# Two schedules for the first projection of a fused decoder trunk: which engine sums the early modulation columns, and in which order the V items run

## The reference, cut to what matters

```python
mod = silu(c) @ ada_w[l] + ada_b[l]                  # (1, 6*1024): shift, scale, gate, twice
sh1, sc1, g1, sh2, sc2, g2 = split(mod, 6)
h = rms_norm(x, norm_mix_g[l]) * (1 + sc1) + sh1     # needs 2048 columns of mod
z = h @ w_in                                         # u, v, bg, cg, hb: 512 columns each
v = layer_norm(gelu(v), ln_g, ln_b)                  # spatial gating unit
s = einsum('hts,bnshd->bnthd', tril(w_s), v) + b_s
```

## Time and profile before

| | |
|---|---|
| median of 3 runs | 1753.85 us (1752.15 to 1755.49) |
| the profiled execution | 1755.49 us |
| its span, first to last instruction | 1753.7 us |
| TensorE busy | 1528.2 us, 87% |
| VectorE busy | 803.5 us, 46% |
| mean granted TensorE clock over the span | 0.939 |

### The profile page before, as it was taken

One profiled execution on the slowest core, in us unless ns is written; L12 is line 12 of the kernel. 1 busy time (PEld: TensorE's weight loads), 2 busy tenths in 40 slices (PEclk: granted clock), 3 DMA queues, 4 the chain that ended last, 5 costly groups with the idle time before them and its releaser, 6 DMA issues. The chain is left out here.

```text
span 1753.7 us, 16992 instructions
## 1 busy us (share of the span) xinstructions
PE 1528.2 (87%) x5419; PEld 847.6 (48%) x5420; DVE 803.5 (46%) x1496; ACT 260.8 (15%) x517; POOL 214.2 (12%) x388
## 2 busy tenths in 40 slices
PE   5989999989965999989579899977998388999992
PEld 3764544458853444444234344432887244444440
DVE  2561786644244233222225999966233522332323
ACT  3210000001131111111131000004112111111113
POOL 2000000000000232312200000000000112233320
PEclk9999999999986999999889999998999589999996
DMA  9553165560155788888462344442003758769866
GB/s 333 177 189 102 65 213 189 178 206 24 49 194 189 203 252 234 263 259 235 95 190 61 84 105 118 115 105 84 24 25 130 278 182 252 212 168 278 259 168 215
DMA packets 194671, 293.99 MB, mean 168 GB/s; under 512 B 11925, under 2 KB 153329, under 8 KB 194624
## 3 DMA queue, kind: packets, MB, share of 16 engines
q1 hardware_dynamic: 172256, 214.33, 38.5%
q0 software_dynamic: 18800, 65.39, 14.8%
q10 hardware_dynamic: 3568, 13.63, 2.1%
HBM read 240.13 MB, written 53.10 MB: 167 GB/s over the span
## 5 line engine op out<-in xcount | busy, mean ns | idle before, releaser
L913 PE MATMUL bank<-HTR,W 128*128 128x512 f32 x1024 | 454.1, 601 | 14.1 <-DVE R L1631 7.2
L1042 PE MATMUL bank<-W,R 128*128 x784 | 354.4, 606 | 23.2 <-DMA W<-in_moe_w_down 19.3
L913 PEld LDWEIGHTS bank<-HTR,W 128*128 128x128 f32 x1024 | 194.4, 192 | 252.4 <-issue 245.6
L1206 DVE TENSOR_TENSOR R<-bank,R 128x256 f32<-128x256 f32 (+1 forms) x91 | 49.3, 542 | 493.6 <-ACT R L706 296.4
L1042 PEld LDWEIGHTS bank<-W,R 128*128 128x128 f32 x784 | 148.5, 195 | 194.5 <-issue 194.5
L991 PE MATMUL bank<-W,R 128*128 128x256 f32 x1024 | 231.8, 385 | 9.0 <-ACT R L810 7.8
L991 PEld LDWEIGHTS bank<-W,R 128*128 128x128 f32 x1024 | 195.1, 193 | 38.7 <-ACT R L810 8.7
L1644 DVE SCALAR_TENSOR_TENSOR R<-R,PT 128x998 f32<-128x998 f32 (+21 forms) x152 | 195.5, 1286 | 5.4
L1057 PE MATMUL bank<-W,R 128*128 x408 | 185.4, 597 | 3.9 <-DVE R L1459 3.9
L1224 DVE SCALAR_TENSOR_TENSOR W<-W,CAB 128x256 f32<-128x256 f32 x280 | 135.7, 485 | 10.0
L1057 PEld LDWEIGHTS bank<-W,R 128*128 128x128 f32 x408 | 74.1, 192 | 78.7 <-issue 78.7
(11 more groups left out here) (200 smaller groups left out, 960.4 us busy)
## 6 DMA issues: line engine op xcount, KB each, us to landing
W<-in_ada_w SPq DMA_DIRECT2D x48, 1024.0 KB, 11.8
W<-in_moe_w_gate SPq DMA_DIRECT2D x32, 1024.0 KB, 6.8
W<-in_moe_w_up SPq DMA_DIRECT2D x32, 1024.0 KB, 11.7
W<-in_moe_w_down SPq DMA_DIRECT2D x32, 1024.0 KB, 14.0
W<-glu_scratch SPq DMA_DIRECT2D x48, 258.0 KB, 4.5
W<-in_conf_w SPq DMA_DIRECT2D x12, 1024.0 KB, 9.1
W<-in_hyb_w_in SPq DMA_DIRECT2D x10, 1024.0 KB, 12.0
xsum_scratch<-X ACTq DMA_DIRECT2D x8, 1024.0 KB, 4.1
```

The source lines that it names most:

```text
L913: ins = pe.matmul(dst[:], lhs(k), rhs(k), start=(k == 0), stop=(k == kc - 1))
L1042: ins = pe.matmul(M[0][:], XT[:, k, :], W[:, bass.ds(at + k * 2 * FE, 2 * FE)], start=(k == 0), stop=(k == KC - 1))
L1206: return dve.tensor_tensor(o, a, b, op)
```

## The change

Three things are edited together.

1. Of the early items, only the odd ones (scale columns) stay on TensorE. The even ones (0, 2, 4, 6) are summed by VectorE with `ada`: item 0 ahead of `rms_apply(0, 0)`, items 2, 4 and 6 in the steps q = 0, 1, 2 ahead of the finishes of that step. `param_columns` stays behind TensorE's first `ada_rows`, which is now that of item 1. The products of all early items go to bank 1.
2. The V groups run weight item by weight item: all 256-token blocks with WV, then all with WV+1. The transposes of the second half of the tokens come ahead of group 2. Four `a` items stand beside WV and four beside WV+1 (none beside WCG), so one is reduced after every V group. In the ring WV+1 moves behind items 8 to 11, and item 15 ahead of WCG.
3. GpSimd no longer waits for the early products before it issues the four loads of the spatial gating unit (256 KB each).

```diff
-    _k = {WV: 3, WV + 1: 4, WCG: 1, WHB: 5, ...}.get(_w, 0)
+    _k = {WV: 4, WV + 1: 4, WHB: 5, ...}.get(_w, 0)
...
-ITEMS += [("w", WV), ("w", WV + 1)] + [("a", n) for n in BESIDE[WV] + BESIDE[WV + 1]]
-for _w in range(WCG, NW0):
+for _w in range(NW0):
     ITEMS += [("w", _w)] + [("a", n) for n in BESIDE[_w]]
-VORDER = [(_j, 2 * _h + _n) for _h in range(2) for _j in range(2) for _n in range(2)]
...
-USED0 = [GROUPS["v"] + 6, GROUPS["v"] + 8]
-USED0 += [GROUPS[_g] + 4 * (_j + 1) for _g in ("cg", "hb", "bg", "u") for _j in range(2)]
+USED0 = [GROUPS[_g] + 4 * (_j + 1) for _g in ("v", "cg", "hb", "bg", "u") for _j in range(2)]
...
 def by_pe(n):
-    return n < NADA0
+    return n < NADA0 and n % 2 == 1
...
-            pool.wait_ge(ada_mm, NADA0)
             pool.dma_start(SGW, i["sgu_w"][0].rearrange("h t s -> t h s")).then_inc(sgu_in, 16)
...
             for q in range(4):
-                ada_rows(2 * q)
+                ada_rows(2 * q + 1)
                 if q == 0:
                     param_columns()
                 transposes(0, 0, ks=(2 * q, 2 * q + 1))
                 reduce_ada(2 * q)
-                ada_rows(2 * q + 1)
                 reduce_ada(2 * q + 1)
-            for m, (j, n) in enumerate(VORDER):
...
+            def v_of(g, w, n):
+                if g == GROUPS["v"] + 2:
                     transposes(0, 1)
                 ht_ready(0, n // 2)
-                rows_of(GROUPS["v"] + m, HTR, slot(at), n)
...
+                rows_of(g, HTR, w, n)
+            for j in range(2):
+                item0(WV + j, GROUPS["v"] + 4 * j, v_of)
+                if j == 0:
                     sgu_columns()
...
             def ada(n):
                 at = item_at("a", n)
                 wait_item(dve, at)
-                dve.wait_ge(red, n - 1)
+                if n == 0:
+                    dve.wait_ge(ca_ok, 1)
+                    dve.wait_ge(pt_ok, 4)
+                if n >= 2:
+                    dve.wait_ge(red, n - 1)
...
+            ada(0)
             rms_apply(0, 0)
             for q in range(4):
+                if q < 3:
+                    ada(2 * q + 2)
                 ada_finish(2 * q)
                 ada_finish(2 * q + 1)
                 evict_ht(0, 0, 0, 0, (2 * q + 1,))
```

More of the change, by code:

```diff
@@ L56 @@
 for _w in range(NW0):
-    _k = {WV: 3, WV + 1: 4, WCG: 1, WHB: 5, WHB + 1: 5, WBG: 5, WBG + 1: 5, WU: 4, WU + 1: 4, NW0 - 1: 4}.get(_w, 0)
+    _k = {WV: 4, WV + 1: 4, WHB: 5, WHB + 1: 5, WBG: 5, WBG + 1: 5, WU: 4, WU + 1: 4, NW0 - 1: 4}.get(_w, 0)
     BESIDE.append(list(range(_n, _n + _k)))
@@ L118, in by_pe @@
 def by_pe(n):
-    return n < NADA0
+    return n < NADA0 and n % 2 == 1
 def summed(n):
-    return n - NADA0 + 1
+    return n // 2 + 1 if n < NADA0 else n - NADA0 // 2 + 1
 def emptied(g):
@@ L386, in wait_used @@
             if kind == "a" and by_pe(n):
-                eng.wait_ge(ada_mm, n + 1)
+                eng.wait_ge(ada_mm, n // 2 + 1)
             elif kind == "a":
@@ L736, in x_pieces, with rows_out @@
                                    scale=RSTD[:, b:b + 1]).then_inc(xn_ok, 1)
-            def rows_out(n):
-                act.wait_ge(ada_mm, n + 1)
-                if n >= 2:
+            def rows_out(k):
+                n = k + 1
+                act.wait_ge(ada_mm, n // 2 + 1)
+                if n >= 3:
                     act.wait_ge(red, n - 1)
[L744 to L748, removed]
+                act.activation(ACC[1], M[1][:, 0:QW], ACT.Copy).then_inc(rows_ev, 1)
             rms_sums(0, 0)
-            evict_ht(0, 0, 0, 0, both_rows_out)
+            evict_ht(0, 0, 0, 0, rows_out)
             rms_sums(0, 1)
-            for m, (j, n) in enumerate(VORDER):
-                if m == 4:
+            for n in range(8):
+                if n == 2:
                     evict_ht(0, 0, 0, 1)
-                c, b = QW * j, 2 * n
+                c, b = QW * (n // 4), 2 * (n % 4)
                 act.activation(V[:, b:b + 2, c:c + QW],
-                               take(GROUPS["v"] + m)[:].rearrange("p (b c) -> p b c", b=2),
+                               take(GROUPS["v"] + n)[:].rearrange("p (b c) -> p b c", b=2),
                                ACT.Gelu).then_inc(free["A"], 1)
@@ L846, in ada_rows @@
                 wait_item(pe, item_at("a", n))
-                if n == 0:
+                if n == 1:
                     pe.wait_ge(ca_ok, 1)
-                elif n >= 2:
-                    pe.wait_ge(rows_ev, n - 1)
+                else:
+                    pe.wait_ge(rows_ev, n // 2)
                 w = slot(item_at("a", n))
@@ L853, in ada_rows @@
                     c = 32 * (k % 4)
-                    ins = pe.matmul(M[1 + n % 2][c:c + 32, 0:QW], CAB[:, k, :], w[:, k, :], start=(k < 4),
+                    ins = pe.matmul(M[1][c:c + 32, 0:QW], CAB[:, k, :], w[:, k, :], start=(k < 4),
                                     stop=(k >= 4))
@@ L860, in reduce_ada @@
                 if by_pe(n):
-                    pe.wait_ge(rows_ev, n + 1)
+                    pe.wait_ge(rows_ev, n // 2 + 1)
                 else:
@@ L865, in reduce_ada @@
                     pe.wait_ge(pt_ok, 4)
-                    pe.wait_ge(const, 12)
                 elif n == 1:
                     pe.wait_ge(ca_ok, 1)
+                    pe.wait_ge(const, 12)
                 else:
@@ L1093, in _ @@
                 reduce_ada(2 * q)
-                ada_rows(2 * q + 1)
                 reduce_ada(2 * q + 1)
[L1097 to L1100, removed]
+            def v_of(g, w, n):
+                if g == GROUPS["v"] + 2:
                     transposes(0, 1)
                 ht_ready(0, n // 2)
-                rows_of(GROUPS["v"] + m, HTR, slot(at), n)
-                for a in beside_of(WV + m // 4, m % 4):
-                    reduce_ada(a)
-                if m == 5:
+                rows_of(g, HTR, w, n)
+            for j in range(2):
+                item0(WV + j, GROUPS["v"] + 4 * j, v_of)
+                if j == 0:
                     sgu_columns()
@@ L1555, in _ @@
             for n in range(8):
-                if n == 4:
+                if n == 2:
                     evict_ht(0, 0, 0, 1)
-                if n == 7:
+                if n == 5:
                     dve.wait_ge(sgt_ps, 1)
@@ L1563, in _ @@
             for b in range(NB):
-                dve.wait_ge(free["A"], emptied(GROUPS["v"] + VORDER.index((1, b // 2))))
+                dve.wait_ge(free["A"], emptied(GROUPS["v"] + 4 + b // 2))
                 link(dve.bn_stats(BST[:, b, :], V[:, b, :]))
```

## The result

| | before | changed |
|---|---|---|
| median of 4 runs each | 1753.15 us | 1768.18 us (1767.42 to 1769.46) |
| span of the profiled execution | 1753.7 us | 1766.3 us |
| ratio, 95% interval | | 1.0087 [1.0072, 1.0103] |

The changed kernel is slower by 12.6 to 18.1 us. The forecast was 1765.6 us, 11.7 above before, in a range from 1756.0 to 1770.0.

What follows compares the result with a forecast made beforehand. The edited part was taken as one serial chain: 57.2 (first V product) + 73.7 + 0.85 + 27.7 = 159.5 us against 147.80, +11.7, giving a median of 1765.6 us, range 1756.0 to 1770.0.

Steps and rivals of the forecast that it cites:

- the mark at the second cg item: Start of the second cg item, by which everything is paid or earned: 159.5 us against 147.80, bounds 152.4 and 161.8.
- T0: First stage, end of `rms_apply(0, 0)`: 28.2 us instead of 19.45, since `ada(0)` waits for item 1; bounds 26.7 and 29.7.
- the V stage: First V product to the cg stage: 73.7 us before the clock allowance, including a new wait after group 0.
- clock term: V stage, allowance for TensorE's slow clock after the stall: 0.85 us, bounds 0 and 1.7.
- the rounds: First stage, T0 to first V product: three serial rounds with an `ada`, a fourth without; 29.0 us instead of 23.6.
- the cg item: First cg item: 27.7 us, with the 4.92 us hole and its 1.7 us of slow clock gone.
- quarter share: First stage: spatial loads run at a quarter rate, delaying item 1 about 1.5 us; equal turns would cost nearer 3.0.
- the slow pace: Rounds: TensorE stays at the 1.2 GHz level because it idles 5.5 us each round; otherwise 4.7 us less.
- The stall: V stage, after group 0: TensorE waits 3.4 us for `ada(8)`, which ends 12.0 us after V's start.
- Faster: Rival: early loads pay and VectorE's sums are free; V starts before 46 us, time 1747.2 us; chance 0.04.
- Given back later: Rival: TensorE's 6.6 us of `ada` waits between 175 and 330 us vanish, leaving +5.1 us; chance 0.09.
- WCG late: Rival: WCG still lands late, so the cg gain of 6.6 us is lost, 1772.2 us; chance 0.08 including longer slow clock.

Runs made afterwards that it cites:

- second profile: The changed kernel unaltered, run and profiled once more with more rounds; ratio to the kernel before 1.0069, second cg item at 161.16 us.
- e3: The kernel before with only the first part of the change, even early items summed on VectorE; ratio 1.0084, first V product at 55.76 us.
- e5: The changed kernel with the four spatial loads held back until the four early products; ratio to the kernel before 1.0069, second cg item at 156.70 us.
- e4: The kernel before with only the third part of the change, GpSimd's four spatial loads issued at once; ratio 1.0003.
- e6: The changed kernel with a third sum buffer, so early sums wait for the reduction three items back; ratio to the kernel before 1.003.
- e7: The changed kernel with three added unused products in each of rounds 1 to 3, in TensorE's gaps; ratio to the kernel before 1.006.
- e12: The changed kernel with 3, 4 and 1 items beside WV, WV+1 and WCG, none beside the first V group; ratio to the kernel before 1.0059.
- e1: The kernel before with only the second part of the change, the V order with four items beside WV and four beside WV+1; ratio 0.9993.
- e2: The kernel before with the new V order, but 3, 4 and 1 items beside WV, WV+1 and WCG, none beside the first group; ratio 0.997.

## Why the prediction was right

**The bound.** Reading the early part as one chain, with the mark at the second cg item, held: the forecast mark was 159.5 and the measured one 159.53, with 161.16 in the second profile. Against the earlier trace rows that is +11.7 and +13.4. The mechanism was right; that the sum met the first mark so closely is luck. T0 came 1.4 us later than forecast, the V stage with its clock term was 1.0 us shorter, and the rounds and the cg item were 0.1 each shorter.

**T0, the end of the scalings.** Forecast 28.2 with bounds 26.7 and 29.7; measured 29.56 (26.82 + 2.74). The chain item 1, columns, copies, `ada(0)`, scalings is in the timeline in that order, and from item 1's first product to T0 it took the 11.1 us of the forecast. That TensorE, and with it `ada(0)`, begins with item 1 instead of item 0 costs 3.5 us of T0 (15.83 in e3 for 12.34); no run moves `param_columns` ahead of item 1 by itself, where it would not wait for that.

The term that was off is what the spatial loads take from item 1. I took a quarter share and 1.5 us, and it was 2.8 us (landing 16.7 us after issue for 13.9 in e5), or 3.1 in e4. The quarter share was a misreading of the earlier trace rows. The DMA issues, in KB and us from issue to landing, of the kernel before, then of the changed one:

```profile
R<-in_conf_ln_b POOLq DMA_DIRECT2D x1, 4.0 KB, 5.3
R<-in_sgu_w POOLq DMA_DIRECT2D x1, 256.0 KB, 6.0
R<-in_sgu_ln_b POOLq DMA_DIRECT2D x1, 256.0 KB, 6.9
R<-in_sgu_b POOLq DMA_DIRECT2D x1, 256.0 KB, 9.8
...
R<-in_sgu_w POOLq DMA_DIRECT2D x1, 256.0 KB, 6.6
R<-in_sgu_b POOLq DMA_DIRECT2D x1, 256.0 KB, 7.6
```

A load of 4 KB from this queue took 5.3 us too, so some 5 of the 11.7 us say little of the share that the loads had of the engines. The 6.4 us that are left for 1 MB are half the rate and not a quarter (an estimate: 11.7 less 5.3, beside the 3.0 us at the full rate). In the changed kernel the four loads were issued from 8.79 us, and the last landed at 18.2, just as item 1 did. The Trainium skill, page "DMA: Bandwidth & Descriptors", section "Queues, rings and completion order", says that each DMA engine takes turns between the queues that have work for it. I had set the result by equal turns aside for the quarter share; the trace fits it, though it does not show the turns themselves.

**The rounds.** Forecast 29.0 us; measured 28.86 (29.56 to 58.42), at the slow pace as chosen. e6 shows that the wait on `red` makes them serial, e7 that the slow level belongs to TensorE's gaps. The choice of the slow pace was partly luck: it counted 5.5 us of idling in each round, and the engine idled 2.65, since `ada_rows` and the second reduction run under VectorE's sum. No row on record then showed what 2.65 us of idling gives, and the fast pace would have put the mark 4.7 us earlier. The Trainium skill, page "TensorE: Matmul & The Clock Gate", section "Part 1: The HAM clock gate", says that activity is what releases the clock; e7's transposes, 1.97 us before the added work and 1.04 after it, agree.

**The V stage.** Forecast 73.7 + 0.85; measured 73.56, and 75.04 (58.57 to 133.61) where the clock fell behind the stall: of the bounds 0 and 1.7 for that term the lower and nearly the upper were seen. The stall is at the place that was named and ends 11.7 us after V's start (forecast 12.0), but group 0 took 9.2 us instead of 8.6, so it idles 2.54 us, not 3.4. The term is worth 2.2 us when removed (e12), since the slow start that it covered then shows.

**The cg stage.** Forecast 27.7 without a wait; measured 27.55. e1 and e2 show the gain apart from the rest.

**To the end.** The shift reached the end. Measured over all runs it is 1.0087 and 1.0069, 12 to 15 us, where the mark gives 11.7 to 13.4. The measured median, 1768.18, is 2.6 us over the forecast and lies in the range only by the 2.5 us that were added to the sum's bounds; in the second set the difference, 12.1 us, is close to the forecast's 11.7. Whether the stages behind cg add a microsecond or two is open: from cg2 to the end of the span the eight kernels with the early sums took 1603.1 to 1608.9 us, mean 1606.3, and the six without 1603.2 to 1606.2, mean 1605.1. The difference of 1.2 us is smaller than the scatter within each set, and its cause, if it has one, is open.

**The rivals.** Faster: its own condition, V before 46 us, was missed by 12 us. Given back later: TensorE's waits for `ada` between 175 and 330 us were the same 6.6 us (3.8 and 2.8) in e3 and, behind its stall, in the changed kernel, and nothing was given back. WCG late: it landed at 117.7 us, 14 us ahead of its use (forecast 18).

## What to carry to other kernels

An engine that is idle by its busy share is free only for work that nothing behind it in its own queue is waited for: the 4 us sums cost their full length on the chain, since the normalisation, the finishes and the evictions stood behind them, and their own buffer made them wait as well. Ask of each moved operation what is queued behind it and whose release it waits for. And do not place a reduction where its sum cannot be ready: the order of the V groups was worth 6.8 us, and one item beside the first group took nearly all of that away.

## What the runs showed of the hardware that I had not expected

Four loads of 256 KB from GpSimd's queue, issued from 8.79 to 10.62 us among SyncE's loads, put an item of 1 MB back by 2.8 us (e5) and 3.1 us (e4), all of the 3.0 us that their bytes need at 352 GB/s. And TensorE stayed at its slow pace through three rounds with 5.33 us of work in 8.0 us and gaps of only 2.65 us each. After idling 2.3 to 2.5 us it came back at either level, from one execution of the changed kernel to another, and the profile's clock column said 1.00 for as long as the engine had not yet run fast.
